# Gated delta heads: scores made once per head, and beta folded into the decay masks

## The reference, cut to what matters

```python
decay = jnp.exp(jnp.where(incl, gc[..., :, None] - gc[..., None, :], -jnp.inf))
kk = jnp.einsum('bnhid,bnhjd->bnhij', k, k)
A = jnp.where(strict, beta[..., :, None] * kk * decay, 0.0)
...
sol = lax.linalg.triangular_solve(A, rhs, left_side=True, lower=True, unit_diagonal=True)
...
qk = jnp.einsum('bnhid,bnhjd->bnhij', q, k) * decay
```

## Time and profile before

| | us |
|---|---|
| three runs: lowest, median, highest | 3524.77, 3526.81, 3535.01 |
| span of the profiled execution, first to last instruction | 3522.0 |
| PE busy in it | 3233.2 (92%) |
| DVE busy in it | 1688.4 (48%) |
| ACT, POOL busy in it | 1099.4 (31%), 248.0 (7%) |
| mean granted TensorE clock | 0.959 |

### The profile page before, as it was taken

One profiled execution on the slowest core, in us unless ns is written; L12 is line 12 of the kernel. 1 busy time (PEld: TensorE's weight loads), 2 busy tenths in 40 slices (PEclk: granted clock), 3 DMA queues, 4 the chain that ended last, 5 costly groups with the idle time before them and its releaser, 6 DMA issues. The chain is left out here.

```text
span 3522.0 us, 38723 instructions
## 1 busy us (share of the span) xinstructions
PE 3233.2 (92%) x15292; PEld 2364.5 (67%) x15292; DVE 1688.4 (48%) x2481; ACT 1099.4 (31%) x1673; POOL 248.0 (7%) x193
## 2 busy tenths in 40 slices
PE   6899999878798899999988899999999988899997
PEld 3476576446643478887745688878888764478886
DVE  3757877584400264424467444334432345644423
ACT  3334232262200232212226333223222223632222
POOL 3201200000100110001020100010000011010001
PEclk8999999989799999999999999999999998999998
DMA  2212110342489622222100232223222210022221
GB/s 93 87 61 72 61 49 24 107 145 96 171 319 420 264 96 97 99 99 110 60 7 1 97 107 95 96 72 112 100 98 72 108 66 1 37 84 96 98 100 52
DMA packets 67120, 354.69 MB, mean 101 GB/s; under 512 B 8896, under 2 KB 9408, under 8 KB 29616
## 3 DMA queue, kind: packets, MB, share of 16 engines
q1 hardware_dynamic: 66992, 352.93, 27.2%
HBM read 349.53 MB, written 2.33 MB: 100 GB/s over the span
## 5 line engine op out<-in xcount | busy, mean ns | idle before, releaser
L469 PE MATMUL psum<-next_x_hi,next_w_hi 128*128 128x512 f32 x1408 | 554.0, 393 | 19.2 <-PEq L68 18.2
L469 PE MATMUL psum<-next_x_lo,next_w_hi 128*128 128x512 f32 x1408 | 551.6, 392 | 0.0
L469 PE MATMUL psum<-next_x_hi,next_w_lo 128*128 128x512 f32 x1408 | 551.3, 392 | 0.0
L399 DVE TENSOR_TENSOR next_w_lo<-next_raw,next_w_hi 128x2048 fp32r<-128x2048 f32 x128 | 293.5, 2293 | 455.1 <-ACT next_w_hi L361 455.1
L361 ACT ACTIVATE next_w_hi<-next_raw 128x2048 fp32r<-128x2048 f32 x128 | 245.3, 1916 | 568.9 <-PE psum L469 552.8
L105 PE MATMUL psum<-mix_normed,mix_ring 128*128 128x512 f32 x832 | 363.5, 594 | 9.8 <-ACT recurrences_work L1124 7.1
L469 PEld LDWEIGHTS psum<-next_x_hi,next_w_hi 128*128 128x128 f32 x1408 | 266.8, 190 | 77.4 <-issue 20.7
L469 PEld LDWEIGHTS psum<-next_x_lo,next_w_hi 128*128 128x128 f32 x1408 | 266.7, 189 | 56.3 <-issue 1.0
L469 PEld LDWEIGHTS psum<-next_x_hi,next_w_lo 128*128 128x128 f32 x1408 | 266.6, 189 | 56.2
L105 PEld LDWEIGHTS psum<-mix_normed,mix_ring 128*128 128x128 f32 x832 | 156.1, 190 | 203.8 <-issue 203.2
L469 PE MATMUL psum<-ffn_hid_hi,next_w_hi 128*128 (+1 forms) x704 | 273.9, 389 | 0.0
(11 more groups left out here) (528 smaller groups left out, 5412.6 us busy)
## 6 DMA issues: line engine op xcount, KB each, us to landing
next_raw<-w_ffn SPq DMA_DIRECT2D x128, 1024.0 KB, 4.9
mix_ring<-w_experts SPq DMA_DIRECT2D x48, 1024.0 KB, 13.6
mix_ring<-w_mix SPq DMA_DIRECT2D x32, 1024.0 KB, 7.1
experts_slabs<-w_experts SPq DMA_DIRECT2D x23, 1024.0 KB, 13.8
mix_normed<-w_experts SPq DMA_DIRECT2D x22, 1024.0 KB, 13.7
mix_ring<-w_gdn SPq DMA_DIRECT2D x16, 1024.0 KB, 4.9
mix_ring<-w_ssd SPq DMA_DIRECT2D x10, 1024.0 KB, 5.0
mix_ring<-decay_rows SPq DMA_DIRECT2D x32, 256.0 KB, 5.6
```

The costliest lines, as they stand in the source:

```text
L399: dve.tensor_tensor(w_lo[:, at(q), :], raw[:, at(q), :], w_hi[:, at(q), :].bitcast(F32), ALU.subtract)\
L469: ins = pe.matmul(out, wp[:, at(q), w], xp, start=start and a == 0, stop=stop and a == 2)
```

## The change

1. `tokens` on TensorE multiplies the keys of each head with themselves, two sets of four products into banks 2 and 3, instead of the keys with the beta-weighted keys, four sets of four into banks 0 to 3. It no longer waits for `kb`.
2. `query_scores` makes two sets of four products instead of four.
3. On VectorE the beta row is multiplied into the decay mask (`weigh_keys`, L1418, written to `kb`) and no longer into the keys; `negate` takes the head's scores times that product. As many operations as before, in another order.
4. Tiles 0 and 1 of the next round no longer wait for `nt_done`, since banks 0 and 1 are not used for scores.

```diff
@@ tile
-                elif p:
+                elif p and at >= 2:
                     pe.wait_ge(nt_done, 4 * (p - 1) + at + 1)
@@ tokens on TensorE
-                for i, (d, hh) in enumerate(chains):
-                    pe.wait_ge(kb_done, 4 * p + i + 1)
+                for hh in range(2):
                     for t in range(NT):
-                        ins = pe.matmul(m.ps[:, i, tok(t)], c[:, 2 + hh, tok(t)], kb[:, i, t, :], start=True,
+                        ins = pe.matmul(m.ps[:, 2 + hh, tok(t)], c[:, 2 + hh, tok(t)], c[:, 2 + hh, tok(t)], start=True,
                                         stop=True)
                     ins.then_inc(scored, 1)
@@ query_scores
-                for i, (d, hh) in enumerate(chains):
+                for hh in range(2):
                     for t in range(NT):
-                        ins = pe.matmul(m.ps[:, 4 + i, tok(t)], c[:, 2 + hh, tok(t)], c[:, hh, tok(t)],
+                        ins = pe.matmul(m.ps[:, 4 + hh, tok(t)], c[:, 2 + hh, tok(t)], c[:, hh, tok(t)],
                                         start=True, stop=True)
@@ tokens on VectorE
-                for i, (d, hh) in enumerate(chains):
-                    dve.wait_ge(kb_in, 16 * 4 * (p + 1))
-                    dve.tensor_tensor(flat(kb[:, i, :, :]), c[:, 2 + hh, :], flat(kb[:, i, :, :]), ALU.mult)\
-                        .then_inc(kb_done, 1)
...
+                def weigh_keys(i):
                     dve.wait_ge(masked, 4 * p + i + 1)
-                    dve.scalar_tensor_tensor(flat(nT[:, i, :, :]), m.ps[:, i, :], -1.0,
-                                             flat(here[:, i, :, :]), ALU.mult, ALU.mult).then_inc(nt_done, 1)
+                    dve.wait_ge(kb_in, 16 * 4 * (p + 1))
+                    dve.tensor_tensor(flat(kb[:, i, :, :]), flat(here[:, i, :, :]), flat(kb[:, i, :, :]), ALU.mult)\
+                        .then_inc(kb_done, 1)
+
+                def negate(i, hh):
+                    dve.wait_ge(scored, 4 * p + hh + 1)
+                    dve.wait_ge(kb_done, 4 * p + i + 1)
+                    dve.scalar_tensor_tensor(flat(nT[:, i, :, :]), m.ps[:, 2 + hh, :], -1.0,
+                                             flat(kb[:, i, :, :]), ALU.mult, ALU.mult).then_inc(nt_done, 1)
```

More of the change, by code:

```diff
@@ L916, in ssd_tile @@
                 pe.wait_ge(landed[s % 2], 16 * (s // 2))
-                if at < 4:
+                if at in (2, 3):
                     pe.wait_ge(nt_done, 4 * (pairs - 1) + at + 1)
-                elif at < 6:
+                elif 4 <= at < 6:
                     pe.wait_ge(silued, round_4 + at - 3)
-                else:
+                elif at >= 6:
                     pe.wait_ge(steps, 28 * pairs + (14 if at < 8 else 28))
@@ L1418, in mask @@
                     ins.then_inc(masked, 1)
-                def negate(i):
-                    dve.wait_ge(scored, 8 * p + i + 1)
+                def weigh_keys(i):
                     dve.wait_ge(masked, 4 * p + i + 1)
-                    dve.scalar_tensor_tensor(flat(nT[:, i, :, :]), m.ps[:, i, :], -1.0,
-                                             flat(here[:, i, :, :]), ALU.mult, ALU.mult).then_inc(nt_done, 1)
+                    dve.wait_ge(kb_in, 16 * 4 * (p + 1))
[6 more added lines that the diff above has]
+                                             flat(kb[:, i, :, :]), ALU.mult, ALU.mult).then_inc(nt_done, 1)
                 for i, (d, hh) in enumerate(chains):
@@ L1428, in tokens @@
                     if i:
-                        negate(i - 1)
-                negate(3)
+                        weigh_keys(i - 1)
+                    if i >= 2:
+                        negate(i - 2, chains[i - 2][1])
+                weigh_keys(3)
+                negate(2, chains[2][1])
+                negate(3, chains[3][1])
                 for i, (d, hh) in enumerate(chains):
@@ L1446, in weigh_scores @@
                 here = decs[p % 2]
-                for i in range(4):
-                    dve.wait_ge(scored, 8 * p + 4 + i + 1)
-                    dve.tensor_tensor(flat(here[:, i, :, :]), flat(here[:, i, :, :]), m.ps[:, 4 + i, :], ALU.mult)\
+                for i, (d, hh) in enumerate(chains):
+                    dve.wait_ge(scored, 4 * p + 2 + hh + 1)
+                    dve.tensor_tensor(flat(here[:, i, :, :]), flat(here[:, i, :, :]), m.ps[:, 4 + hh, :], ALU.mult)\
                         .then_inc(dec_done, 1)
```

## The result

The changed kernel is slower. Over ten runs each, its median is 3541.6 us (3528.3 to 3548.2), that of the kernel before 3523.1 (3520.2 to 3535.0). The ratio of the runs is 1.0041, with a 95% interval of 1.0028 to 1.0055: 14 us, between 10 and 19. The two medians lie 18.5 us apart, near the upper end of it; in the two comparisons further down the median of before was 3526.5 and 3526.0. Two executions of before in those later comparisons were far slower than all others (3817.7 and 6621.0 us) and are left out throughout. The profiled execution of the changed kernel is the slowest of its ten.

The account below looks back on a forecast made before the run. The prediction took TensorE, busy 92% of the span, as the bound, with VectorE not far behind. Rounds 1 to 4 losing 2.0 + 4.5 + 4.5 + 1.4 = 12.4 us took 3526.8 to 3539.2 us; range 3522 to 3550.

Parts of the forecast that it names:

- TensorE's saving: In `tokens` and `query_scores`, half the small products and no `nt_done` wait start tile 2 4.5 us earlier in round 2.
- VectorE's order costs nothing: Inside `tokens`, another operation covers each weighted mask before its use; if wrong, bubbles of 0.1 us in a few places.
- Held operations: In rounds 2 and 3 POOL's earlier additions hold some 12 of VectorE's 30 short operations, making VectorE 7.6 us late.
- the second rival: Each short operation under POOL waits for one addition; VectorE 10 us late in rounds 2 and 3; 3548 us; chance 0.12.
- `out` waits: In rounds 2 and 3 TensorE stands 7 us for `weigh_scores`, then a 1.9 us clock penalty; each 4.5 us later.
- Round 1: First `gdn` round: tile 2 5.5 us earlier, 10 operations held, TensorE stands before `lengths`; round 2.0 us later.
- Round 4: Last `gdn` round, without POOL work: TensorE stands 4 us before tile 8, clock penalty 1.9; inverse 1.4 us later.
- The sum: Over the four `gdn` rounds, 12.4 us later in all, giving a median of 3539.2 us.
- The third rival: No clock penalty after TensorE's pauses: rounds 1 to 4 cost 0.2, 2.6, 2.6 and -0.4; 3532 us; chance 0.13.

Follow-up runs that it names:

- e1: Changed kernel with diag and outer, operands of VectorE's 30 short operations, in PSUM bank 6 instead of SBUF; 3511.7 us, ratio to before 0.9962.
- e4: Changed kernel with seven dummy matmuls between tile 4 and `out` in rounds 2 and 3; 3545.9 us in one run.
- e7: Changed kernel with four dummy matmuls ahead of tile 8 in round 4 alone; 3540.9 us in one run.
- e3: Changed kernel with two dummy matmuls behind the query products in rounds 1 to 3; 3531.0 us in one run.
- e2: Changed kernel with five dummy matmuls behind the query products in rounds 1 to 3; 3523.0 us, ratio to before 0.9989.

## Why the prediction was right

- **TensorE's saving.** Eight products in place of sixteen and no wait for `nt_done`: tile 2 came 4.5 us earlier in rounds 2 and 3, as forecast.
- **VectorE's order costs nothing.** Held; e1, with the same order, shows no lateness.
- **Held operations.** Forecast some 12 of 30 in rounds 2 and 3, and a chain 7.6 us longer. Measured 12, and 18.63 against 11.1. The pattern of one held and one slipping through held for the longer operations too; the second rival, one operation for each addition, fell.
- **`out` waits.** Forecast 7 us, measured 6.6. Rounds 2 and 3: forecast 4.5 longer each, measured 4.1 and 4.6. The clock cost `out` 1.8 and 2.3 us, forecast 1.9.
- **Round 1.** Forecast 2.0 longer, measured 2.0, but by two errors that cancel. Eight operations were held and not ten, so `lengths` waited 3.3 us and not 6, and tile 6 began 0.2 us earlier than before and not 1 later; and the clock cost tiles 6 and 7 2.2 us and not 1. That the sum came out is luck.
- **Round 4.** Forecast 1.4, measured 2.0. The pause was 3.9 us as forecast (4); the clock behind it cost 2.6 us and not 1.9.
- **The sum.** 12.4 forecast, 12.7 in the rounds, 14 (10 to 19) in the runs; median 3539.2 forecast, 3541.6 measured. The forecast stood on a median of before of 3526.8, from three runs, where ten gave 3523.1. There are slips in the working of 0.1 us: from 302.58 to 307.0 are 4.4 us and not 4.5, tile 8 of before comes at 562.9, and the wake-up of ACT is 0.21 us and not 0.15. The first makes the forecast 12.2, the others change nothing.
- **The third rival was mis-sized.** I gave 2.6 us for each of rounds 2 and 3 without a clock penalty, taking all 1.9 us as exposed. In e4, with the clock up at `out`, `lengths` waits for the squares, and tile 6 starts 61.1 us after the transposes where it was 57.8 before: without the penalty the round would still lose 3.3. I had compared TensorE's and ACT's arrival at `lengths` only with the penalty in it.

Round 1 is the same code in the changed kernel, e4 and e7, and took 81.8, 84.3 and 84.1 us in their profiles. Timeline of TensorE in round 1 of e4, to be laid beside the changed kernel's:

```profile
178.63 3.55 PE L933 MATMUL psum<-const_sb,mix_ring 128*128 128x1 f32 x16 [4.67 <-ACT mix_ring L1138]
182.04 16.81 PE L105 MATMUL psum<-mix_normed,mix_ring 128*128 128x512 f32 x32
```

In e4 and e7 nine short operations were held and in the changed kernel eight, and `weigh_scores` began 1.4 and 1.2 us later after the transposes. The rest, 1.1 us, is the lower clock in `lengths` and tiles 6 and 7. So both the number of held operations and the cost of the clock differ between executions of the same code. In round 4 the same pause of 3.9 us ahead of tile 8 cost 2.6 us in the changed kernel, 2.5 in e3 and 1.7 in e2 and e4. What decides it stays open. The spread of the runs does not tell either: the ten of the changed kernel lie within 20 us, and those of before within 15 in the first comparison and within 21 in the later ones.

## What to carry to other kernels

When a step on the busiest engine gets shorter, look at what it releases and over whose work that will now run. Here 4.5 us less on TensorE moved POOL's additions over a chain of short VectorE operations, where each held operation cost 0.95 us, and 32 of them were held in three rounds where 10 had been. Where VectorE's short operations with two inputs in SBUF run beside POOL, give them an operand in PSUM if a bank is free: that cost next to nothing here and turned a loss of 0.4% into a gain of 0.4%. And a pause of the matmul engine costs its length and the slow stretch behind it, unless another engine's chain is the one that ends last there.

## What the runs showed of the hardware

- A short operation of VectorE with two inputs in SBUF that comes while an addition of POOL runs is held, and the next one slips through; with one input in PSUM none is held (0.20 to 0.22 us against 1.15 to 1.22 for 128x48 and its neighbours, e1). The large operations with one input in PSUM took the same under POOL as without it (four of L1454 2.48 us, twelve of L687 7.96 and 7.95, in e1 and the changed kernel).
- POOL is delayed a little too: its 12 additions took 17.12 us where 12 of VectorE's operations were held, 17.03 with nine (e3), 16.87 with four (16.81 in e2), and 16.77 with none (e1).
- The clock can fall without a long pause: a wait of 0.68 us (e4, e3), or of 0.23 (e3, round 1), and then 16 matmuls of one column were followed by the lower clock, tiles 6 and 7 taking 15.7 to 17.0 us. The same 16 matmuls without the wait were followed by 13.98 us for the two tiles.
- A pause of 3.9 to 4.4 us ahead of tile 8 was followed by 1.7 to 3.0 us of loss at the lower clock, one of 6.6 ahead of `out` by 1.8 to 2.4, and one of 4.7 ahead of `lengths` by 4.5 (e4, e7). The same pause in the same code does not always cost the same.
